# Gate and up products of a feed-forward network: three 256-column matmuls per input chunk in place of one of 512 and one of 256

## The reference

```python
def swiglu_ffn(x, g, w_gu, w_down):
    h = rms_norm_2(x, g)
    gate, up = jnp.split(h @ w_gu, 2, axis=-1)
    return (jax.nn.silu(gate) * up) @ w_down
```

## Time and profile before

| | |
|---|---|
| time, median of 3 runs | 2235.34 us (2235.04 to 2235.49) |
| span of the profiled execution | 2233.4 us (its own time around that span isn't given) |
| TensorE matmul | busy 2227.1 us, 100% |
| TensorE weight load | busy 2051.0 us, 92% |
| VectorE | busy 1833.4 us, 82% |
| ScalarE | busy 1131.6 us, 51% |
| read from memory | 405.23 MB, 182 GB/s over the span |

### The profile page before, as it was taken

One profiled execution on the slowest core, in us unless ns is written; L12 is line 12 of the kernel. 1 busy time (PEld: TensorE's weight loads), 2 busy tenths in 40 slices (PEclk: granted clock), 3 DMA queues, 4 the chain that ended last, 5 costly groups with the idle time before them and its releaser, 6 DMA issues.

```text
span 2233.4 us, 42466 instructions
## 1 busy us (share of the span) xinstructions
PE 2227.1 (100%) x16140; PEld 2051.0 (92%) x16140; DVE 1833.4 (82%) x3023; ACT 1131.6 (51%) x1503; POOL 4.8 (0%) x10
## 2 busy tenths in 40 slices
PE   9999999999999999999999999999999999999999
PEld 8998999999998999999999889999999998999998
DVE  8888568888888668887988878888898887888887
ACT  5445465445445565444434676654454446766443
POOL 0000000000000000000000000000000000000000
PEclk9999999999999999999999999999999999999999
DMA  7555445555555435654556443555556555344654
GB/s 253 193 194 208 159 153 198 197 196 171 199 196 207 170 135 189 213 194 163 202 190 206 170 152 125 179 197 190 188 177 207 189 174 189 120 142 166 221 196 133
DMA packets 76817, 407.63 MB, mean 183 GB/s; under 512 B 9264, under 2 KB 9920, under 8 KB 44336
## 3 DMA queue, kind: packets, MB, share of 16 engines
q1 hardware_dynamic: 75792, 404.93, 53.0%
q10 hardware_dynamic: 720, 0.89, 0.1%
q0 software_dynamic: 208, 0.49, 0.1%
HBM read 405.23 MB, written 1.05 MB: 182 GB/s over the span
## 4 chain that ended last, share of the span: by engine, by line
PE 97%; DVE 1%; issue 0%; ACT 0%; DMA 0%; DVEq 0%; SPq 0%; ACTq 0%
PE ps_proj L684 13%; PE ps_aux L693 13%; PE ps_y L263 10%; PE ps_y L264 10%; PE ps_y L265 10%; PE ps_proj L688 7%; PE ps_aux L696 7%; PE ps_proj L1120 4%; PE ps_proj L1127 4%; PE ps_proj L1121 4%; PE ps_proj L263 2%; PE ps_proj L265 1%; PE ps_proj L264 1%; PE ps_aux L651 1%; PE ps_proj L651 1%; PE ps_aux L1941 1%
## 5 line engine op out<-in xcount | busy, mean ns | idle before, releaser
L130 DVE TENSOR_TENSOR w_lo_front<-w_raw_front,w_hi_front 128x2048 fp32r<-128x2048 f32 x238 | 544.0, 2286 | 42.3 <-ACT w_hi_front L105 42.0
L105 ACT CAST w_hi_front<-w_raw_front 128x2048 fp32r<-128x2048 f32 x238 | 452.9, 1903 | 178.0 <-PE ps_aux L696 144.8
L263 PE MATMUL ps_y<-hidden_lo,w_hi_back 128*128 128x256 f32 x1344 | 372.5, 277 | 0.1
L264 PE MATMUL ps_y<-hidden_hi,w_lo_back 128*128 128x256 f32 x1344 | 371.3, 276 | 0.0
L265 PE MATMUL ps_y<-hidden_hi,w_hi_back 128*128 128x256 f32 x1344 | 371.3, 276 | 0.0
L105 ACT CAST w_hi_back<-w_raw_back 128x1024 fp32r<-128x1024 f32 x248 | 259.8, 1048 | 146.4 <-PE ps_y L265 119.8
L887 ACT ACTIVATE silu_gate<-silu_gate 128x256 f32<-128x256 f32 x176 | 73.7, 419 | 508.6 <-DVE silu_gate L924 508.5
L684 PE MATMUL ps_proj<-xt_lo_hi,w_hi_front 128*128 128x512 f32 x1280 | 319.7, 392 | 0.0
L693 PE MATMUL ps_aux<-xt_lo_hi,w_hi_front 128*128 128x512 f32 x1280 | 319.6, 392 | 0.0
L130 DVE TENSOR_TENSOR w_lo_back<-w_raw_back,w_hi_back 128x1024 fp32r<-128x1024 f32 x248 | 302.2, 1218 | 4.0 <-ACT w_hi_back L105 3.3
L684 PEld LDWEIGHTS ps_proj<-xt_lo_hi,w_hi_front 128*128 128x128 f32 x1280 | 228.5, 188 | 39.6
(11 more groups left out here) (462 smaller groups left out, 3826.5 us busy)
## 6 DMA issues: line engine op xcount, KB each, us to landing
w_raw_front<-in_stream SPq DMA_DIRECT2D x251, 1024.0 KB, 4.9
w_raw_back<-in_stream SPq DMA_DIRECT2D x252, 512.0 KB, 3.7
m_rel_bias<-in_rel_bias SPq DMA_DIRECT2D x2, 2048.0 KB, 8.2
m_params<-in_params SPq DMA_DIRECT2D x2, 656.0 KB, 4.2
w_raw_front<-in_stream SPq DMA_DIRECT2D x4, 256.0 KB, 6.6
w_raw_front<-in_stream SPq DMA_DIRECT2D x2, 512.0 KB, 8.8
x<-in_x ACTq DMA_DIRECT2D x3, 256.0 KB, 6.7
out<-x SPq DMA_DIRECT2D x3, 256.0 KB, 2.3
```

What stands on the lines that cost most here:

```text
L105: self.nc.scalar.copy(self.hi[part][:, parity], self.raw[part][:, parity]).then_inc(self.hi_done[part], by)
L130: eng.tensor_tensor(self.lo[part][:, parity], self.raw[part][:, parity], self.hi[part][:, parity].bitcast(F32), ALU.subtract).then_inc(sel ...
L263: nc.tensor.matmul(out, ah, bl, start=start, stop=False)
L264: nc.tensor.matmul(out, al, bh, start=False, stop=False)
```

## The change

Gate and up products no longer use 512-column matmuls. Per input chunk three matmuls of 256 columns go into the first half of the bank: high weights x low input, low weights x high input, high weights x high input. In the loop the eight chunks follow one another, each with all three. So a product is 24 matmuls of 256 columns (it was 8 of 512 and 8 of 256), and both gate and up wait for the low front weights (`split`) before the first one. The start functions change in the same way. As nothing is left in the second half of the bank, VectorE's reductions go: `scale_gate` and `scale_up` multiply straight out of PSUM. In the first slot of a network, where the inverse norms come later, the bank is first copied to SBUF and then scaled in place. The gap ahead of the high front weights grows from 40 to 72 values (128 bytes), and the gap of 32 values behind them goes, so that all other tiles stay where they are.

```diff
-        sb("gap_hi_front", [P, 40], F32)
+        sb("gap_hi_front", [P, 72], F32)
         self.hi = [sb("w_hi_front", [P, 2, 2 * CH], F32R)]
-        sb("gap_hi_back", [P, 32], F32)
...
+def all_three(s, bank, part, k, stop=True):
+    hi, lo = part
+    cols = slice(k * P, (k + 1) * P)
+    out = bank[:, 0:T]
+    s.nc.tensor.matmul(out, hi[:, cols], s.xl[:, k], start=k == 0, stop=False)
+    s.nc.tensor.matmul(out, lo[:, cols], s.xh[:, k], start=False, stop=False)
+    return s.nc.tensor.matmul(out, hi[:, cols], s.xh[:, k], start=False,
+                              stop=stop and k == KD - 1)
...
 def both_high(s, bank, part, k, stop=False):
-    return s.nc.tensor.matmul(bank[:], part[0][:, k * P:(k + 1) * P],
-                              s.xlh[:, k].rearrange("p j t -> p (j t)"), start=k == 0, stop=stop)
+    hi = part[0][:, k * P:(k + 1) * P]
+    s.nc.tensor.matmul(bank[:, 0:T], hi, s.xl[:, k], start=k == 0, stop=False)
+    return s.nc.tensor.matmul(bank[:, 0:T], hi, s.xh[:, k], start=False, stop=stop)
...
 (ffn_up)
-    gate, bank = w.parts(slot, 0), s.pj[slot % 2]
-    pe.wait_ge(w.hi_done[0], base + slot + 1)
-    for k in range(KD):
-        s.nc.tensor.matmul(bank[:], gate[0][:, k * P:(k + 1) * P],
-                           s.xlh[:, k].rearrange("p j t -> p (j t)"), start=k == 0, stop=False)
     pe.wait_ge(w.split[0], base + slot + 3)
-    for k in range(KD):
-        last = s.nc.tensor.matmul(bank[:, 0:T], gate[1][:, k * P:(k + 1) * P], s.xh[:, k],
-                                  start=False, stop=k == KD - 1)
-    w.taken(last, 0)
...
+    for c, bank in enumerate((s.pj[slot % 2], s.pa[slot % 2])):
+        part = w.parts(slot, c)
+        for k in range(KD):
+            last = all_three(s, bank, part, k)
+        w.taken(last, c)
...
 (ffn_first, chunks 2 to 7; ffn_start uses all_three in place of by_both)
-        for bank, part in three:
-            both_high(s, bank, part, k)
-        last_gate = high_low(s, s.pj[0], gate0, k)
-        last_up = high_low(s, s.pa[0], up0, k)
-        last = high_low(s, s.pj[1], gate1, k)
+        last_gate = all_three(s, s.pj[0], gate0, k)
+        last_up = all_three(s, s.pa[0], up0, k)
+        last = all_three(s, s.pj[1], gate1, k)
...
 (ffn_vector)
+    def first_out(to, bank, c, done):
+        w.wait_taken(dve, base, slot0, c)
+        nc.vector.tensor_copy(to[:, 0], bank[:, 0:T]).then_inc(done, 1)
+
+    def first_scale(of, came, done):
+        dve.wait_ge(came, f + 1)
+        nc.vector.tensor_tensor(of[:, 0], of[:, 0], s.py[1][:, 0:T], ALU.mult).then_inc(done, 1)
+
+    def scale_gate(before, k):
+        p = k % 2
         w.wait_taken(dve, base + before, slot0 + k, 0)
+        nc.vector.tensor_tensor(s.act[:, p], s.pj[p][:, 0:T], s.rbc[:], ALU.mult).then_inc(
+            s.gate_scaled, 1)
...
     def step(before, k):
-        add_gate(before, k)
-        scale_gate(before, k, s.rbc[:])
+        scale_gate(before, k)
         back(before, k)
-        add_up(before, k)
-        scale_up(before, k, s.rbc[:])
+        scale_up(before, k)
         hidden(before, k)
```

More of the change, by code:

```diff
@@ L666, in by_high @@
     cols = slice(k * P, (k + 1) * P)
-    nc.tensor.matmul(bank[:, T:2 * T], hi[:, cols], s.xh[:, k], start=k == 0, stop=False)
+    nc.tensor.matmul(bank[:, 0:T], hi[:, cols], s.xh[:, k], start=k == 0, stop=False)
     nc.tensor.matmul(bank[:, 0:T], lo[:, cols], s.xh[:, k], start=False, stop=False)
@@ L680, in ffn_up @@
     pe = s.nc.tensor
-    gate, bank = w.parts(slot, 0), s.pj[slot % 2]
-    pe.wait_ge(w.hi_done[0], base + slot + 1)
-    for k in range(KD):
-        s.nc.tensor.matmul(bank[:], gate[0][:, k * P:(k + 1) * P],
-                           s.xlh[:, k].rearrange("p j t -> p (j t)"), start=k == 0, stop=False)
-    pe.wait_ge(w.split[0], base + slot + 3)
-    for k in range(KD):
-        last = s.nc.tensor.matmul(bank[:, 0:T], gate[1][:, k * P:(k + 1) * P], s.xh[:, k],
-                                  start=False, stop=k == KD - 1)
-    w.taken(last, 0)
[L691 to L698, removed]
+    pe.wait_ge(w.split[0], base + slot + 3)
+    for c, bank in enumerate((s.pj[slot % 2], s.pa[slot % 2])):
[3 more added lines that the diff above has]
+        w.taken(last, c)
 def ffn_first(s, w, base, slot0, n):
@@ L768, in ffn_start @@
     gate1, up1 = w.parts(1, 0), w.parts(1, 1)
-    def high(bank, part, k):
-        s.nc.tensor.matmul(bank[:], part[0][:, k * P:(k + 1) * P],
-                           s.xlh[:, k].rearrange("p j t -> p (j t)"), start=k == 0, stop=False)
-    def low(bank, part, k):
-        return s.nc.tensor.matmul(bank[:, 0:T], part[1][:, k * P:(k + 1) * P], s.xh[:, k],
-                                  start=False, stop=k == KD - 1)
     for _ in range(WARM):
@@ L782, in ffn_start @@
         wait_x(s, 0, k)
-        high(s.pj[0], gate0, k)
+        both_high(s, s.pj[0], gate0, k)
     pe.wait_ge(s.lead_lo, 1)
     for k in range(2):
-        low(s.pj[0], gate0, k)
+        high_low(s, s.pj[0], gate0, k)
     for k in range(2, 4):
         wait_x(s, 0, k)
-        by_both(s, s.pj[0], gate0, k)
+        all_three(s, s.pj[0], gate0, k)
     pe.wait_ge(s.lead_lo, 2)
     for k in range(4):
-        by_both(s, s.pa[0], up0, k)
+        all_three(s, s.pa[0], up0, k)
     pe.wait_ge(s.lead_lo, 3)
@@ L804, in ffn_start @@
     for k in range(KD):
-        high(s.pj[1], gate1, k)
+        both_high(s, s.pj[1], gate1, k)
     pe.wait_ge(s.half_split, HALF_AT[0] + 1)
     for k in range(KD):
-        last = low(s.pj[1], gate1, k)
+        last = high_low(s, s.pj[1], gate1, k)
     w.taken(last, 0)
@@ L812, in ffn_start @@
     for k in range(KD):
-        high(s.pa[1], up1, k)
+        both_high(s, s.pa[1], up1, k)
     pe.wait_ge(s.ident_rounded, 1)
@@ L817, in ffn_start @@
     for k in range(KD):
-        last = low(s.pa[1], up1, k)
+        last = high_low(s, s.pa[1], up1, k)
     w.taken(last, 1)
@@ L988, in ffn_vector @@
         inverse(s, n)
-    add_gate(0, 0)
-    add_up(0, 0)
+    first_out(s.act, s.pj[0], 0, s.gate_added)
+    first_out(s.hid, s.pa[0], 1, s.up_added)
     dve.wait_ge(s.rows_done, spread_count(n))
-    scale_gate(0, 0, s.py[1][:, 0:T])
-    scale_up(0, 0, s.py[1][:, 0:T])
+    first_scale(s.act, s.gate_added, s.gate_scaled)
+    first_scale(s.hid, s.up_added, s.up_scaled)
     hidden(0, 0)
```

34 lines of the change are left out of this document (5 added, 29 removed).

## The result

The changed kernel took 2238.8 us (median; nineteen executions between 2230.9 and 2252.11) against 2235.06 us (2234.32 to 2235.71) for the kernel before: ratio 1.0026, 95% interval 1.0017 to 1.0034. It is slower by 0.26% by that ratio (the two medians lie 3.7 us apart, 0.17%), where I had forecast 0.27% faster. The times of the kernel before lie within 1.4 us; those of the changed kernel fall into heaps: 3 executions at 2231 to 2233 us, 8 at 2237 to 2239, 6 at 2244 to 2246, 2 at 2251 and 2252. The heaps are some 6.4 us apart. (A twentieth execution, in the slow state with a granted clock of 0.555, took 3707.21 us and is left out.) The profiled execution belongs to the third: 2246.22 us, span 2244.4.

What follows compares the result with a forecast made beforehand. TensorE was taken as the bound, busy 2227.1 of 2233.4 us. The terms -8.7 - 0.9 + 6.0 - 2.3 - 1.4 + 1.3 gave -6.0 us, so 2229.3 us (0.27% faster), range 2225 to 2242.

Steps and rivals of the forecast that it cites:

- The loop (-8.7): Gate and up products in the loop: 320 products at 2.720 us instead of 2.747, -8.7 us.
- The new wait (+6.0): Third slot of each network: TensorE waits for VectorE's split of the low front weights, +6.0 us, bounds 3 and 7.9.
- Waits that go (-2.3 and -1.4): Third and fourth slots, and last two down products: TensorE's waits for late hidden values vanish, -2.3 and -1.4 us.
- outside the loop (-0.9): The 32 gate and up products outside the loop change in the same way, -0.9 us.
- the one on the gap: High front weights' place: the new gap puts all four weight tiles at 288, counted for the fast pace; no separate term.
- Slow steps after the new wait (+1.3): Behind the third slot's wait: 40 steps, each 4.2 ns slower, in eight networks, +1.3 us.
- I take 0, and 2 us for the range: Mixer streams, whose front weights move too: 0.1 us per 24 steps to either side, taken as 0.
- Rival 1: Gate, up and down all keep the slow pace, 0.1175 us a step: +42 us, 2277 us; chance 0.10.
- rival 2: Half-way: the loop falls to the slow pace at times, mean near 0.1145: 2238 us, 2234 to 2242; chance 0.17.
- Rival 3: Each of 2560 added matmuls costs 4.2 ns: +11 in place of -8.7, 2249 us; chance 0.05.
- Rival 4: The new wait is small, 3 us, and leaves no slow steps: 2225 us; chance 0.11.
- Rival 5: The waits don't go, TensorE again in step with VectorE: 2.3 + 1.4 stay, 2233 us; chance 0.10.

Runs made afterwards that it cites:

- the layout at 224: Changed kernel with gaps of 56 and 16 values, high front weights at 224 bytes past a multiple of 512, other weight tiles at 288: 2291.22 us, ratio 1.0249.
- the order without the wait: Changed kernel with gate's high products in the loop first, in 256 columns, waiting for the high parts alone: 2244.52 us, ratio 1.0044.

## Why the prediction was wrong

**The loop (-8.7).** Right: 8.160 us a slot in every free network. Two products less by 0.053 us a slot are -8.5 us over 160 slots. The rule of the Trainium skill cited ahead (TensorE: Matmul & The Clock Gate, Back-to-back issue gap), which the section gives for a matmul in isolation, would have made this +6.4; the free networks don't show that. 512 columns were dearer than by the rule (0.2294 us), as the earlier trace rows had it.

**The new wait (+6.0).** Right in place, releaser and size. VectorE's timeline at the second network's start, for the earlier trace rows:

```profile
358.51 0.42 DVE L892 TENSOR_TENSOR silu_gate<-silu_gate,ps_y 128x256 f32<-128x256 f32 x1 [0.27 <-PE ps_y L607]
...
362.08 2.29 DVE L129 TENSOR_TENSOR w_lo_front<-w_raw_front,w_hi_front 128x2048 fp32r<-128x2048 f32 x1
```

The first scaling is held by the norm's rows (L607), as predicted. The split ends at 364.37, TensorE starts at 364.42. From the last matmul before to the first one behind, less one step, the eight waits are 1.15, 0.83, 0.64, 0.83, 0.20 and three times 0.83 us: 6.1. I had forecast 1.15, three times 0.82, 0.25 and three times 0.70. The page's 4.8 us of idle time is the same thing, measured from modelled ends, which take 0.16 us off each. Taking the wait away, and the slow slots behind it, gave 6.0 us.

**Waits that go (-2.3 and -1.4), outside the loop (-0.9).** With the old gaps the first down product and the loop together changed by 5.4 - 9.5 = -4.1 us. The pace is -8.5 of that. The waits of that run, measured as above, are +5.4 (1.18 us in the first network, 0.33 in the fifth, 0.65 in the others), and its third slots are 1.3 us longer than 8.16 in all. That leaves some -2.2 for the waits that went (unrounded), forecast -2.3; it is a remainder, not measured apart. The last two down products fell by 1.38. The stages between fell by 0.4 instead of 0.9. So the near hit of this run is in part luck: the new wait was 0.6 us cheaper there than forecast, the stages between gave 0.5 us less.

**The step that failed** is the one on the gap. It stood in two places. "One thing more for it: the high front weights begin 160 bytes past a multiple of 512 ... the new gap puts all four at 288, where the back stream of rows 5 ran fast": this took a stream of before, where the front lay elsewhere, as evidence for a layout in which all four weight tiles share a place. In the earlier trace rows the back stream was fast with the high front at 160; after the move the same stream, whose own tiles stayed, is slow. And "I take 0, and 2 us for the range" for the mixers: the new gap costs them 3.8 us (871.24 against 867.46 in the run with the old gaps).

**Slow steps after the new wait (+1.3).** "Streams of 256-column matmuls leave the slow pace after some 10 to 45 steps" is true for the old gap: there the slow entry into the second network ends after some 50 steps, and in the others after two or three. The term's size came out by luck: the third slots of that run are 1.3 us over 8.16 in all, but 0.9 of it is the first step behind the wait, 0.22 us instead of 0.11 in every network. With all four weight tiles at one place the slow pace needn't end at all: over 1,400 steps in the fourth network. The held networks cost 12.6 us in the profiled execution and, if the heaps are what I take them for, near 6.3 in the median one. With the old gaps' -5.6 and the mixers' 3.8 that makes +4.5 us; the medians differ by 3.7.

**The rivals.** Rival 1 came nearest: all streams are of one form, no 512-column run stands between to break the slow pace, and one product of that form left in the slot does break it (2233.47 us). It lacked the condition: with the old gaps the slow pace ends without such a run. I priced it for all eight networks at once (+39 us for the loop's three products) and gave it 0.10; the layout at 224 shows about that, +40.5 us in the loop. What I didn't see is the state in between: a network at a time, by chance. The time then fell into rival 2's band (2234 to 2242), but not for its reason: no network's loop runs half-way, it is at 8.16 or 8.48. Rival 3, a price for each matmul, is refuted by the free networks' 8.16. Rival 4 is refuted by the waits' 6.1 us. Rival 5 is refuted: the last two down products lost their wait.

**What stays open.** Shown: the losses come with the place of the high front against the tiles behind it; 256 bytes apart is as bad as none; 224 is worst, where the front is both 64 bytes from the other weights and 256 from the input; moving by 128 bytes the high front, the low front, both fronts or both backs lets no network be held; and the slow pace goes on while every other engine and the DMA are idle. For 512-column steps it is the high front against the input. Not shown for 256: which reads of TensorE meet, two weight tiles' or a weight tile's and the input's; why the slow pace, once entered, stays; whether another engine takes part in setting it off; and which network falls into it in which execution. The input tile was never moved by itself; that run would part the two readings of 224. The mixers' pace isn't explained by the fronts' place alone: both fronts at 160 slow it, both at 288 with the backs at 160 don't.

## What to carry to other kernels

A change of a tile's place is a change of its own: time it apart from the code that comes with it. Here the new products with the old gaps were worth -6 us and the 128 bytes of padding +10 us. When a stream has two paces, ask not only what each costs but whether it can get out of the slow one, in the layout after the change; and where times fall into heaps, divide the distance between heaps by the number of slots. A stream of matmuls near the bound is worth trying with a weight tile 128 bytes off the others: of five such layouts here four lost nothing, and the fifth (both fronts moved) 5 us.

## What the runs showed of the hardware

- Steps of 256-column matmuls with changing weights have two paces at the same granted clock (1.000): 0.1133 and 0.1178 us (slots of 8.160 and 8.480 us). Either can last a whole network of 160 us. Which of them depends on where the tiles begin in their partition: with all four weight tiles equal, or the high front 256 bytes off, held at times (2 and 3 of 8 networks in the traces); with the high front 64 bytes off the other weights and 256 off the input, held always; with one or two weight tiles 128 bytes off the rest, never in any of five layouts.
- 512-column steps slow down too, from 0.2294 to 0.2327 us, when the high front moves by 128 bytes. A run of them reads only the high front and the input, and its steps repeat to 1 ns whatever the other engines do.
- The slow pace needs no other engine: nine steps from 910.38 us on take 0.1178 us each with VectorE, ScalarE, GpSimd and DMA idle. By the Trainium skill (SBUF — State Buffer, Who interferes with whom) TensorE never waits on any other engine. The trace agrees for this stretch; what TensorE's pace does depend on is where its own tiles lie, from 8.16 to 8.48 us a slot.
- The slow pace is entered behind a wait (0.67 us idle in the fourth network) or out of a slow stretch before the loop (third network of the order without the wait), and a single product with 512-column matmuls in each slot is enough for it not to last (8.213 us a slot in all eight networks).
